# A decoder block with expert retrieval on one core: six places for gathered rows in place of eight, and residual rows and scores that stay on chip

## The reference

```
xn  = rmsnorm(x)
mix = (sigmoid(g_sb) * (stickbreaking(xn) @ W_sb)
     + sigmoid(g_ml) * (mlstm(xn) @ W_ml)) @ w_out
h   = x + mix
hn  = rmsnorm(h)
# PEER, 8 heads: two sets of 128 keys, the best 16 of each, the best 16 of their 256 sums
s1, s2 = (hn @ w_query) . keys1, keys2          # 16 x 128 scores for each token
e, gate = top 16 of (top16(s1) + top16(s2)), softmax
y   = h + sum over 128 experts of gate * gelu(u[e] . hn) * v[e]
out = rmsnorm(y)
```

## Time and profile before

| | us |
|---|---|
| median of 3 runs | 3311.7 (3311.04 to 3311.96) |
| profiled execution | 3315.3 |
| its span, first to last instruction | 3313.1 |
| PE busy | 2620.7 (79%) |
| DVE busy | 2081.0 (63%) |
| POOL busy | 1216.3 (37%) |
| ACT busy | 1114.8 (34%) |
| moved by DMA | 1272 MB, of it gathered rows 1074 MB |

### The profile page before, as it was taken

One profiled execution on the slowest core, in us unless ns is written; L12 is line 12 of the kernel. 1 busy time (PEld: TensorE's weight loads), 2 busy tenths in 40 slices (PEclk: granted clock), 3 DMA queues, 4 the chain that ended last, 5 costly groups with the idle time before them and its releaser, 6 DMA issues.

```text
span 3313.1 us, 40476 instructions
## 1 busy us (share of the span) xinstructions
PE 2620.7 (79%) x14560; PEld 1321.6 (40%) x14560; DVE 2081.0 (63%) x4806; ACT 1114.8 (34%) x3524; POOL 1216.3 (37%) x1048
## 2 busy tenths in 40 slices
PE   8998888998888788997878778998785555555555
PEld 6775534564454344553444334454351111111111
DVE  1324668677568877775458888675449656765444
ACT  3212335342332643322323554332222222222222
POOL 0001334333334543433334554333334444444443
PEclk9999999999999989999889989999998777767777
DMA  4356999999999999999999999999999999999997
GB/s 136 114 159 234 417 394 368 416 399 407 388 417 417 410 398 417 418 417 416 412 417 414 410 389 418 418 418 416 414 415 408 414 420 421 416 418 413 421 420 325
DMA packets 224535, 1272.03 MB, mean 384 GB/s; under 512 B 24912, under 2 KB 26960, under 8 KB 93264
## 3 DMA queue, kind: packets, MB, share of 16 engines
q0 software_dynamic: 147456, 1073.81, 78.8%
q1 hardware_dynamic: 64128, 161.56, 13.3%
q10 hardware_dynamic: 12752, 34.08, 2.6%
HBM read 1256.78 MB, written 12.58 MB: 383 GB/s over the span
## 4 chain that ended last, share of the span: by engine, by line
DMA 39%; PE 37%; DVE 8%; ACT 6%; issue 6%; POOL 3%; POOLq 0%; DVEq 0%; ACTq 0%; SPq 0%
DMA rowsb<-uv,e_idx 37%; PE yacc L889 14%; PE mixp L586 9%; DVE rowsb L1688 4%; POOL rowsb L958 3%; PE mixp L611 2%; PE mixp L648 2%; PE mixp L637 2%; ACT diag L1261 2%; ACT wg L1256 2%; PE mixp L598 2%; DMA wt<-w_query_ 1%; PE yacc L586 1%; DVE area L1355 1%; DMA wt<-w_merge 1%
## 5 line engine op out<-in xcount | busy, mean ns | idle before, releaser
L958 POOL DMA_INDIRECT rowsb<-uv,e_idx x1024 | 1212.1, 1184 | 2068.9 <-PE yacc L889 1610.1
L1688 DVE CUSTOM_DVE_ANT_0 rowsb<-rowsb,hnrow 128x1024 f32<-128x1024 f32 x1024 | 1241.6, 1223 | 868.2 <-DMA rowsb<-uv,e_idx 866.9
L889 PE MATMUL yacc<-rowsb,diag 64*64 64x512 f32 x8192 | 1219.6, 719 | 635.9 <-ACT diag L1261 626.7
L889 PEld LDWEIGHTS yacc<-rowsb,diag 64*64 64x64 f32 x8192 | 298.6, 150 | 1380.5 <-ACT diag L1261 950.1
L1242 ACT ACTIVATE gmt<-dots 128x2 f32<-128x2 f32 x512 | 104.2, 203 | 1676.7 <-DVE dots L1688 1675.7
L586 PE MATMUL mixp<-area,wt 128*128 128x256 f32 x2144 | 499.1, 387 | 1.8 <-ACT area L1022 1.2
L586 PEld LDWEIGHTS mixp<-area,wt 128*128 128x128 f32 x2144 | 401.5, 192 | 131.3 <-issue 80.8
L1261 ACT ACTIVATE diag<-ident,wg 128x64 f32<-128x64 f32 x1024 | 300.3, 340 | 16.7
L1256 ACT ACTIVATE wg<-gmt,gate 128x1 f32<-128x1 f32 x1024 | 245.6, 286 | 17.7
L976 ACT ACTIVATE area<-mixp 128x512 f32<-128x512 f32 (+3 forms) x334 | 148.4, 488 | 282.4 <-PE mixp L586 163.5
L611 PE MATMUL mixp<-area,wt 128*128 128x256 f32 x960 | 226.5, 390 | 10.2 <-DMA wt<-w_query_ 8.7
(11 more groups left out here) (216 smaller groups left out, 1758.4 us busy)
## 6 DMA issues: line engine op xcount, KB each, us to landing
wt<-w_merge SPq DMA_DIRECT2D x96, 512.0 KB, 7.9
wt<-w_feat SPq DMA_DIRECT2D x80, 512.0 KB, 7.9
wt<-w_query_ SPq DMA_DIRECT2D x64, 512.0 KB, 12.3
wt<-w_tok SPq DMA_DIRECT2D x32, 512.0 KB, 11.3
wt<-w_out_ SPq DMA_DIRECT2D x32, 512.0 KB, 7.9
rowsb<-uv,e_idx POOLq DMA_INDIRECT x1024, 13.7
area<-x_rows ACTq DMA_DIRECT2D x4, 1024.0 KB, 13.3
area<-keysT ACTq DMA_DIRECT2D x16, 256.0 KB, 11.9
```

What stands on the lines that cost most here:

```text
L889: last = pe.matmul(yacc[at:at + HP, k % 2, c * NCH:(c + 1) * NCH], diag[r * HP:(r + 1) * HP, s, :], rowsb[r * HP:(r + 1) * HP, s, D + c * ...
L958: pool.indirect_dma_start(rowsb[:, n % RS, :], None, uv, bass.IndirectOffsetOnAxis(ap=e_idx[:, i % 2, k:k + 1], axis=0)).then_inc(row_load ...
L1688: dve.tensor_tensor_reduce(rowsb[:, s, 0:D], rowsb[:, s, 0:D], hnrow[:, i % HR, :], 1.0, 0.0, ALU.mult, ALU.add, dots[:, s:s + 1]).then_in ...
```

## The change

`RS` goes from 8 to 6, which frees 16 KB in each partition. `acc7` (4 KB) and `sc` (8 KB) are replaced by `hres`, three tiles of rows (12 KB), and `scores`, two tiles of scores (16 KB). Tile i uses `hres[i % 3]` and `scores[i % 2]`.

The sum h is written straight into `hres`; the norms, the retrieval's addition and the output's store all work there. The stores and loads of `h_scratch` and of `sc_scratch` are gone with their waits. Before the sum of block b > 0 DVE waits until tile 2b-2 has been stored. The second tile's scores are copied from PSUM into their own tile by the same ACT instruction that filled `scst`. Tile 0's norm, scaling and store stand in slots 3, 5 and 7 like those of the other tiles. Since 128 is no multiple of 6, places are counted by the running number of the row over all tiles.

```diff
-        RS = 8
+        RS = 6
-        sc = sb("sc", [P, QT, NKEYS])
+        scores = sb("scores", [P, 2, QT, NKEYS])
-        acc7 = sb("acc7", [P, D])
+        hres = sb("hres", [P, HR, D])
...
-                def load_scores(i, g):
-                    b = i // NT
-                    act.wait_ge(experts_ready, 4 * (i - 1) + g + 1)
-                    if i > 1 and g == 0:
-                        act.wait_ge(ss7_ready, i - 1)
-                    act.wait_ge(sc_stored[g % 2], 16 * (2 * b + g // 2 + 1))
-                    act.dma_start(sc[:, 4 * g:4 * g + 4, :].rearrange("p q k -> p (q k)"),
-                                 sc_dram[i][:, 4 * g * NKEYS:4 * (g + 1) * NKEYS]).then_inc(sc_loaded[g], 16)
-                def load_h(i):
-                    act.wait_ge(h_stored[i], 16)
-                    if i > 0:
-                        act.wait_ge(o7_stored, 16 * i)
-                    act.dma_start(acc7[:, :], h_dram[i * P:(i + 1) * P, :]).then_inc(h7_loaded, 16)
...
                             if k == 0:
-                                emptied(act, ("o", b, 2 * t + 1))
-                                act.dma_start(h_dram[(t0 + t) * P:(t0 + t + 1) * P, :], ht[:, t, :]).then_inc(h_stored[t0 + t], 16)
+                                for c in range(2):
+                                    emptied(act, ("o", b, 2 * t + c))
...
-                            act.dma_start(sc_dram[t0 + 1][:, g * NCH:(g + 1) * NCH], scst[:, g % 2, :]).then_inc(sc_stored[g % 2], 16)
...
-                            if b > 0 or g > 1:
-                                act.wait_ge(sc_stored[g % 2], 16 * (2 * b + g // 2))
+                            if b > 0:
+                                act.wait_ge(experts_ready, 4 * t0)
+                                act.wait_ge(ss7_ready, t0 - 1)
                             for t in range(NT):
                                 key = ("sc", b, g, t)
-                                if t == 0:
-                                    ...
-                                    keep(key, wide[:, g * NCH + lo:(g + 1) * NCH], B(bank(key))[:, lo:NCH])
-                                else:
-                                    keep(key, scst[:, g % 2, :], B(bank(key)))
+                                lo = 2 * P if (b, g, t) == (0, 0, 0) else 0
+                                keep(key, wide[t][:, g * NCH + lo:(g + 1) * NCH], B(bank(key))[:, lo:NCH])
...
-                        if i == 1 and p == 19:
-                            act.wait_ge(experts_ready, 8)
-                        if i > 0 and p == (19 if i == 1 else 3):
+                        if i > 0 and p == 3:
                             norm(i - 1)
-                        if i > 0 and p == (23 if i == 1 else 7):
+                        if i > 0 and p == 7:
                             store_out(i - 1)
-                        if p == (36 if i == 1 else 20):
-                            load_h(i)
...
                             dve.wait_ge(xrow_loaded, 16 * (b + 1))
+                            if b > 0:
+                                dve.wait_ge(o7_stored, 16 * (t0 - 1))
                             ready(dve, ("o", b, 3))
                             for n in range(4):
-                                own = ht[:, n // 2, n % 2 * NCH:(n % 2 + 1) * NCH]
-                                dve.scalar_tensor_tensor(own, X[:, n, :], 0.5, own, ALU.mult, ALU.add).then_inc(x_taken[n], 1)
+                                at = slice(n % 2 * NCH, (n % 2 + 1) * NCH)
+                                dve.scalar_tensor_tensor(hres[:, (t0 + n // 2) % HR, at], X[:, n, :], 0.5, ht[:, n // 2, at],
+                                                         ALU.mult, ALU.add).then_inc(x_taken[n], 1)
```

More of the change, by code:

```diff
@@ L167, in build @@
         SBA_AREA = [(rem_early, left_early, wT_early, mask_early, N)] + [(rem, left, wT, mask, T)] * (NB - 1)
-        sc = sb("sc", [P, QT, NKEYS])
-        wide = sc[:, :, :].rearrange("p q k -> p (q k)")
-        cand = wide.rearrange("p (h c) -> p h c", h=PH)
-        eq = wide.rearrange("p (n a) -> p n a", a=TOPK)
+        scores = sb("scores", [P, 2, QT, NKEYS])
+        wide = [scores[:, u, :, :].rearrange("p q k -> p (q k)") for u in range(2)]
         v16 = sb("v16", [P, PH, 2, TOPK])
@@ L1013, in mix @@
                         if k == 2:
-                            if b > 0:
-                                for i in range(t0 - NT, t0):
-                                    act.wait_ge(h_stored[i], 16)
-                            else:
+                            if b == 0:
                                 act.wait_ge(vec_loaded, 16)
@@ L1207, in mix @@
                             keep(key, qT[:, 0:2, :], X[:, 0, :].rearrange("p (c t) -> p c t", c=2))
-                            keep(("sc0", 0), wide[:, 0:2 * P], X[:, 0, 0:2 * P])
+                            keep(("sc0", 0), wide[0][:, 0:2 * P], X[:, 0, 0:2 * P])
                         if k >= 4 and k % 4 == 0:
@@ L1265, in norm @@
                     act.wait_ge(y7_ready, 2 * (i + 1))
-                    act.activation(wide[:, 0:D], acc7[:, :], ACT.Square, accum_out=ss7[:, 0:1]).then_inc(ss7_ready, 1)
+                    act.activation(wide[0 if i == 0 else (i + 1) % 2][:, 0:D], hres[:, i % HR, :], ACT.Square, accum_out=ss7[:, 0:1]).then_inc(ss7_ready, 1)
                     act.wait_ge(ss7_ready, i + 1)
@@ L1283, in _ @@
                         spread(i, p)
-                        if i == 1 and p == 19:
-                            act.wait_ge(experts_ready, 8)
-                        if i > 0 and p == (19 if i == 1 else 3):
+                        if i > 0 and p == 3:
                             norm(i - 1)
-                        if i > 0 and p == (23 if i == 1 else 7):
+                        if i > 0 and p == 7:
                             store_out(i - 1)
-                        if p == (36 if i == 1 else 20):
-                            load_h(i)
-                        if i == 0 and p in SCORES_AT:
-                            load_scores(1, SCORES_AT.index(p))
-                        if i > 0 and i % NT == 0 and p == 12:
-                            for g in range(4):
-                                load_scores(i + 1, g)
                         for b in range(NB):
@@ L1363, in sba @@
                             ready(dve, ("sbv", b, NT - 1))
-                            if b > 0:
-                                for u in range(2):
-                                    dve.wait_ge(sc_stored[u], 16 * 2 * b)
                             mark(dve.memset(left[:, span:span + 1], 1.0))
@@ L1586, in top_parts @@
                     g = first // 2
+                    sc = scores[:, i % NT, :, :]
+                    cand = wide[i % NT].rearrange("p (h c) -> p h c", h=PH)
+                    eq = wide[i % NT].rearrange("p (n a) -> p n a", a=TOPK)
                     if (i, first, count) == (0, 0, 1):
                         emptied(dve, ("sc0", 0))
-                    elif i % NT == 0:
-                        emptied(dve, ("sc", i // NT, g, 0))
                     else:
-                        dve.wait_ge(sc_loaded[g], 16 * (i // NT + 1))
+                        emptied(dve, ("sc", i // NT, g, i % NT))
                     after_marks()
@@ L1701, in residual @@
                             own, far = slice(q * HP, (q + 1) * HP), slice((1 - q) * HP, (2 - q) * HP)
-                            last = dve.tensor_tensor(acc7[own, at], acc7[own, at], yacc[far, 1, at], ALU.add)
+                            last = dve.tensor_tensor(own_h[own, at], own_h[own, at], yacc[far, 1, at], ALU.add)
                         last.then_inc(y7_ready, 1)
                 def final_norm(i):
+                    own_h = hres[:, i % HR, :]
                     dve.wait_ge(std7_ready, i + 1)
@@ L1732, in _ @@
                             gates(*GATES[GATES_AT[i * PP + p - 1]][1:])
-                        if i > 0 and p == (21 if i == 1 else 5):
+                        if i > 0 and p == 5:
                             final_norm(i - 1)
```

43 lines of the change are left out of this document (14 added, 29 removed).

## The result

| | before | changed |
|---|---|---|
| median of 4 runs each, same chip | 3311.8 | 3473.4 (3466.7 to 3481.8) |
| ratio | | 1.0487, 95% interval 1.0473 to 1.0501 |
| profiled execution | 3315.3 | 3478.1 |
| moved by DMA | 1272 MB | 1255 MB |

The forecast was 3326 us with a range up to 3358. The direction was right; the loss was eleven times the one forecast (14) and lies outside the range.

What follows compares the result with a forecast made beforehand. The prediction took the DMA engines, full at about 418 GB/s after the head, as the bound. From 3311.7 us, 49 for places plus 3 for the wait less 37.6 for transfers gave 3326 us, range 3292 to 3358.

Steps and rivals of the forecast that it cites:

- Two places less: Gathered rows: issued two row times later, they lose time only below a 5.4 us floor; 49 us lost, 1 in quiet stretches.
- two dips: Shallow dips at 2500:2610 and 2640:2670, priced at 2.7 and 0.9 us.
- The third rival: Quiet stretches after 2500 us run dry too: 63 us more, 3389 us; chance 0.05.
- The dips: Eleven stretches where DVE or TensorE was late: six deep cost 33.5 us, five shallow 10.7, repeats 5 more.
- the first rival: The dips are compute's, so places waiting for DVE or TensorE are no use: loss only 18 us, 3295 us; chance 0.24.
- Floor: Least time from a gather's issue to its landing on an empty queue: 5.4 us, ends 4.8 and 6.5.
- The transfers that go: Residual and score stores and loads, 16.8 MB, 15.7 of them after the head: 37.6 us gained at 418 GB/s.
- The new wait: DVE waits 9.8 us at block 2's sum for tile 2's store: cost 3 us, 0 at the other sums.
- Moves: Tile 0's norm in earlier slots and second-tile scores copied to another address: 0 us, ends -4 and +4.
- The sum: Whole kernel: 49 + 3 - 37.6 + 0 = +14.4 us, giving 3326 us.

Runs made afterwards that it cites:

- the seven-place kernel: The kernel before with seven places for gathered rows in place of eight, all else as it was: 3333.0 us, ratio 1.0049.
- Gathers alone: A kernel of nothing but 1.05 MB gathers, a set number in flight: 2.49 us a row with 8 to 4, 2.71 with 3, 2.95 with 2, 5.80 with 1.
- Gathers in pairs with a use on three engines: Only gathers, each place held by DVE's product, two ACT copies and 1 to 3 matmuls: eight places 2.50 to 2.51 us a row, six 2.73 to 2.92.
- The run with eight places from tile 6 on: The changed kernel with two more row places in the mixer's work area from tile 6 on: 3381.8 us, ratio 1.0216.
- Six places alone: The kernel before with six places for gathered rows, residual rows and scores still through DRAM: 3485.8 us, ratio 1.0529.
- three variants of the changed kernel: The changed kernel with a pair's rows finished one by one (3461.2 us), with eight places from tile 6 on (3381.8), or with finished tiles stored earlier (3457.4).
- row by row release: The changed kernel with TensorE finishing and counting the first row of a pair before the second: 3461.2 us, ratio 1.0453.

## Why the prediction was wrong, point by point

**Two places less: the failed step.** It said that "the many rows near 10.7 stay above the floor, so it costs only 1 us there". It took 5.4 us as a hard floor: as long as a row takes longer than that, the engines are full. What failed is this pricing of the overlap. Two places cost 175 us for 49, and 98 us in the last 320 rows of the changed kernel for 1 and two dips. Its own numbers, turned into rows in flight and set beside the curve measured afterwards, show why. A time from issue to landing, divided by the row time, is how many gathers are in flight: 12.3 / 2.52 = 4.9 before, (12.3 - 2.5) / 2.52 = 3.9 with seven places, 7.3 / 2.52 = 2.9 with six. Gathers alone give 2.49 us a row at 4 and 5 in flight and 2.71 at 3. So 4.9 is safe, 3.9 is at the edge (the seven-place kernel loses 16 us in all), and 2.9 has fallen off. In the new trace the product of a pair's first row starts 8.4 us after its issue and that of the second 9.3, which is 3.0 and 3.3 times 2.85.

320 rows by 0.22 us from that curve alone would have been 70 us; it was 98. Gathers in pairs with a use on three engines are slower than the curve too, 2.7 to 2.9 us with six places, so the difference needs nothing else of the block. The run with eight places from tile 6 on shows the same from the other side: 421 GB/s again.

The third rival had the place and the sign of this (quiet stretches, 63 us) and a chance of 0.05. It was argued away because the one row of 6.5 us had weights beside it. The test named for it, a DMA share below 0.97 in the last 400 us, came out at 0.96.

**The dips.** Predicted 49 in eleven dips, 45 of them before the middle of tile 5. Six places alone cost 69 us there, spread over all eleven half tiles with 2 to 13 us each. Set beside before row by row, 40 of the 69 come in the nine dips named or within 15 us behind them, most in three places: 8 around 855:885, 12 in 1080:1180, 12 around 1890:1955. In 450:560, 640:700 and 700:775 together only 3.5 come, where 16 were priced; for the last two that fits the first rival's reading, that TensorE was the one to wait for. The other 29 us come between the dips, where the prediction priced nothing. Weights share the engines in these stretches, so gathers in flight alone don't tell how full they are, and no run took the two apart. The gathers of tiles 0 and 1 end 17 us later, as the test for this step wanted; tiles 6 and 7 should have stayed within 3 and lose 79.

**Floor.** The trace's 5.4 stands: alone and with no other traffic a gather takes 5.3 to 5.7 us. The Trainium skill's page DMA: Bandwidth & Descriptors, section Anatomy of one DMA (SWDGE path), makes 4.4 of it (estimate by its 2.0 us plus bytes over 436 GB/s); the run lies 0.9 to 1.3 above, and the measured figure decides. It is a sum for one DMA alone. Either number leads to the same miss, because the step that failed is on several in flight.

**The transfers that go.** Right at a full queue: 16 us for 8.4 MB and 12 us for 4.2 MB, by 418 GB/s 17.6 (without the two stores in the head) and 10. With six places the edits bring 14 us in all, plus or minus 8. Put back the new wait's 5 and the rest is 19, for a predicted 37.6. That saved bytes are worth less where the queue is too short to keep the rate up fits this, but no run shows it by itself, and three variants of the changed kernel stand 12 to 13 us lower than it before tile 6.

**The new wait.** Right: the place, its releaser and its length, 10.7 us at block 2's sum for 9.8. Its price is about 5 by the traces for 3, within the 2.1 to 5.6 given. The other sums do not wait.

**Moves.** Priced at 0; no run separates them.

**The sum**, by ratios, with the wait from the traces and the transfers as what is left over: places 175 predicted as 49, wait 5 as 3, transfers -19 as -37.6; 161 against 14. The direction was right, since the places do cost more than the transfers bring. Where they cost it, and how much, was not.

**The first rival** (the dips are compute's, 3295) falls as a whole: the places alone cost 69 us up to the middle of tile 5, where it allowed 18, though its reading of 640:700 and 700:775 fits. A landed row that waits for TensorE is no loss of itself, but it holds the place of the next gather.

## What to carry to other kernels

Turn every depth of a queue into transfers in flight (time from issue to landing over time per transfer) and compare it with a measured curve of rate over transfers in flight; the landing time on an empty queue is no threshold. A transfer place that is held by its use counts for nothing in flight: with 4.6 to 6.3 us of use and pairs, six places were about three. The curve of gathers alone is the best case: pairs and uses make it worse (four places with the shortest use have 2.5 in flight on average by their landings and took 3.11 us a row; two single gathers in flight took 2.95). On-chip room that takes places from a gather must be priced by the knee: the eighth place was worth 16 us here, the seventh 159, and room that is free anyway (the last block's work area) gave 12 us for nothing.

## What the runs showed of the hardware

- The DMA share hides a slow queue. With 2 gathers in flight it reads 0.97 while the rate is 357 of 422 GB/s, 15% less; with 3 it reads 0.99 at 389. Busy time of the engines includes packets that take longer: in that kernel the mean 8 KB packet took 313 ns with 4 in flight, 334 with 3 and 355 with 2, while the median stayed between 309 and 312, so that a few long ones make the difference. GB/s beside the share shows it, and in the changed kernel it did (0.96, 369).
- 4 gathers of 1.05 MB in flight reach 422 GB/s, and 8 move no more; one alone moves 182.
- The matmuls of two rows on different quarters of the array end together, whichever row comes first in the list: in the timeline of row by row release the count after the first row came 0.1 us before that after the second, of 3.7 us.
